# Layer 3's gated linear attention: decay product first, second values and keys turned inside the gate products, filling steps ahead of the squares' sum

## The reference

```
gate_logit = b_lr @ w_a2 + b_a2
log_a = log_sigmoid(gate_logit) / 16
b = cumsum(log_a within a chunk);  b_last, b_ref = b at the chunk's end, at its middle
qe = q * 128**-0.5 * exp(b - b_ref);  ke = k * exp(b_ref - b)
o_intra = (causal part of qe @ ke.T) @ v
chunk_kv = (k * exp(b_last - b)).T @ v
state[n+1] = exp(b_last) * state[n] + chunk_kv[n]
o = o_intra + (q * 128**-0.5 * exp(b)) @ state
b_out = rmsnorm(o) * b_norm_g * silu(b_gate)
y = concat(a_out, b_out) @ w_out
```

## Time and profile before

| | |
|---|---|
| median of 3 runs | 3675.92 us (3673.31 to 3685.54) |
| the profiled execution's own time | 3676.82 us |
| its span, first to last instruction | 3674.7 us |
| mean granted TensorE clock | 0.968 of full speed |
| TensorE busy | 3449.6 us in 16240 matmuls |
| VectorE, ScalarE, GpSimd busy | 1772.1, 1119.6, 1071.0 us |
| the four heads' part of the span | about 3067 to 3500 us |

### The profile page before, as it was taken

One profiled execution on the slowest core, in us unless ns is written; L12 is line 12 of the kernel. 1 busy time (PEld: TensorE's weight loads), 2 busy tenths in 40 slices (PEclk: granted clock), 3 DMA queues, 4 the chain that ended last, 5 costly groups with the idle time before them and its releaser, 6 DMA issues.

```text
span 3674.7 us, 39245 instructions
## 1 busy us (share of the span) xinstructions
PE 3449.6 (94%) x16240; PEld 2811.3 (77%) x16240; DVE 1772.1 (48%) x1897; ACT 1119.6 (30%) x1492; POOL 1071.0 (29%) x1144
## 2 busy tenths in 40 slices
PE   9989999999999999898898999999999999999997
PEld 7655678888887688555598989989987777777776
DVE  4567562222223688686455544545574223443522
ACT  4333352111122522444531111111243332322442
POOL 3111343323233243000023433433342222211243
PEclk9999999999999999899899999999999999999998
DMA  3000211111111211000111111111121111001232
GB/s 122 23 23 29 103 63 63 52 46 49 50 46 64 87 46 41 12 6 6 59 41 39 43 46 52 41 46 52 41 87 52 64 59 45 29 24 35 75 133 96
DMA packets 56249, 192.21 MB, mean 52 GB/s; under 512 B 6900, under 2 KB 7284, under 8 KB 55560
## 3 DMA queue, kind: packets, MB, share of 16 engines
q1 hardware_dynamic: 56072, 189.71, 15.0%
HBM read 172.83 MB, written 16.86 MB: 52 GB/s over the span
## 4 chain that ended last, share of the span: by engine, by line
PE 78%; DVE 14%; ACT 5%; issue 2%; DMA 0%; POOL 0%; DVEq 0%; ACTq 0%; SPq 0%; POOLq 0%
PE psum L270 21%; PE psum L271 21%; PE psum L272 21%; PE psum L138 11%; DVE mix L107 3%; DVE work L98 2%; PE psum L312 2%; PE psum L314 1%; PE psum L313 1%; DVE res L98 1%; DVE res L107 1%; ACT L126 1%; DVE work L116 1%; DVE u_padded L98 1%; ACT work L126 1%
## 5 line engine op out<-in xcount | busy, mean ns | idle before, releaser
L98 POOL TENSOR_TENSOR w_lo<-w_raw,w_hi 128x256 fp32r<-128x256 f32 x1140 | 1070.8, 970 | 2569.0 <-ACT w_hi L131 2569.0
L270 PE MATMUL psum<-x_hi,w_hi 128*128 128x512 f32 (+2 forms) x3264 | 1220.2, 374 | 31.0 <-issue 6.8
L271 PE MATMUL psum<-x_lo,w_hi 128*128 128x512 f32 (+2 forms) x3264 | 1179.0, 361 | 0.0
L272 PE MATMUL psum<-x_hi,w_lo 128*128 128x512 f32 (+2 forms) x3264 | 1174.9, 360 | 0.0
L131 ACT CAST w_hi<-w_raw 128x1024 fp32r<-128x1024 f32 x285 | 298.2, 1048 | 1585.0 <-PE psum L272 1521.8
L270 PEld LDWEIGHTS psum<-x_hi,w_hi 128*128 128x128 f32 x3264 | 623.0, 191 | 128.2 <-issue 34.2
L271 PEld LDWEIGHTS psum<-x_lo,w_hi 128*128 128x128 f32 x3264 | 622.3, 191 | 84.3 <-issue 19.1
L272 PEld LDWEIGHTS psum<-x_hi,w_lo 128*128 128x128 f32 x3264 | 620.9, 190 | 71.4
L270 PE MATMUL psum<-h_hi,w_hi 128*128 128x512 f32 x848 | 337.4, 398 | 15.3 <-issue 9.0
L272 PE MATMUL psum<-h_hi,w_lo 128*128 128x512 f32 x848 | 331.8, 391 | 0.0
L271 PE MATMUL psum<-h_lo,w_hi 128*128 128x512 f32 x848 | 331.8, 391 | 0.0
(11 more groups left out here) (281 smaller groups left out, 3675.6 us busy)
## 6 DMA issues: line engine op xcount, KB each, us to landing
w_raw<-w_dram SPq DMA_DIRECT2D x285, 512.0 KB, 3.2
res<-spill SPq DMA_DIRECT2D x4, 1044.0 KB, 9.5
res<-x_dram SPq DMA_DIRECT2D x8, 512.0 KB, 8.3
res<-x_dram SPq DMA_DIRECT2D x4, 1024.0 KB, 8.0
spill<-res SPq DMA_DIRECT2D x1, 4096.0 KB, 13.9
spill_a<-mix SPq DMA_DIRECT2D x8, 512.0 KB, 2.6
res<-spill_a SPq DMA_DIRECT2D x8, 512.0 KB, 4.7
x_plain<-spill SPq DMA_DIRECT2D x4, 1024.0 KB, 10.2
```

What stands on the lines that cost most here:

```text
L98: self.mark(self.e.tensor_tensor(out, a, b, op), inc)
L270: t.e.matmul(out, whi, xhi, start=k == 0, stop=False, skip_group_check=True)
L271: t.e.matmul(out, whi, xlo, start=False, stop=False, skip_group_check=True)
L272: ins = t.e.matmul(out, wlo, xhi, start=False, stop=last_k, skip_group_check=True)
```

## The change

TensorE issues a head's decay product ahead of the transposes of the first values. The second values are transposed after 32 of the 48 filling steps and the keys after 40. ScalarE has the products of a new label, ("first gate", h), ahead of its copies of the second values and keys, and the rest of the three products behind them. Of the ten steps behind the squares' sum, four stand ahead of its wait. Two functions, `uses` and `claim_banks`, are added to the core and called nowhere.

```diff
-    FILL_V, FILL_NORM, FILL_SGU, FILL_FIRST, FILL_STEP, FILL_ROOT = 4, 2, 4, 3, 2, 10
+    FILL_V, FILL_NORM, FILL_SGU, FILL_FIRST, FILL_STEP, FILL_SUM, FILL_ROOT, FILL_TURN, FILL_KEYS = 4, 2, 4, 3, 2, 4, 6, 32, 8
...
         for h in range(H3):
-            t.wait_ge(*k.products["bv", 2 * h].freed)
-            t.wait_ge(self.vt_ready, 16)
-            t.wait_ge(self.o_out, 8 * h)
-            t.wait_ge(self.state, 15 * h)
-            self.pe_turn(t, self.v_f, 3 * h)
             fill = self.pe_values_and_gates(t, h)
             t.wait_ge(self.w_a2_landed, 16)
             t.wait_ge(self.biased, 9)
             t.wait_ge(*k.products["lr",].freed)
             t.wait_ge(self.b_out, 2 * h)
             t.mm([(ps[:, 4 + i, :], self.w_a2[:, h, :], self.lr[0:16, i * 512:(i + 1) * 512], True, True) for i in range(2)], self.gate_mm)
+            t.wait_ge(*k.products["bv", 2 * h].freed)
+            t.wait_ge(self.vt_ready, 16)
+            t.wait_ge(self.o_out, 8 * h)
+            t.wait_ge(self.state, 15 * h)
+            self.pe_turn(t, self.v_f, 3 * h)
+            advance(fill, self.FILL_TURN)
+            k.label(("first gate", h))
+            t.wait_ge(*k.products["bv", 2 * h + 1].freed)
+            self.pe_turn(t, self.v_f, 3 * h + 1)
+            advance(fill, self.FILL_KEYS)
+            t.wait_ge(self.q_ready, 4 * h + 4)
+            self.pe_turn(t, self.kd, 3 * h + 2)
             drain(fill)
             k.label(("values", h))
-            t.wait_ge(*k.products["bv", 2 * h + 1].freed)
-            self.pe_turn(t, self.v_f, 3 * h + 1)
-            t.wait_ge(self.q_ready, 4 * h + 4)
-            self.pe_turn(t, self.kd, 3 * h + 2)
             self.pe_update(t, h, 0)
...
+            advance(fill, self.FILL_SUM)
             t.wait_ge(self.o_total, h + 1)
             t.wait_ge(self.masked, 16 * h + 16)
             t.mm(k.ones_of(self.ke, TWO, (4, 5)), self.o_sum)
...
-            self.act_products(a, ("values", h))
+            self.act_products(a, ("first gate", h))
             self.act_turned(a, self.v[1], 3 * h + 1)
             self.act_turned(a, self.kd_tok, 3 * h + 2)
+            self.act_products(a, ("values", h))
```

More of the change, by code:

```diff
@@ L297, in claim_at, with uses, claim_banks @@
         return p, before
+    def uses(self, *slots):
+        return [(self.slots[i], self.slot_uses[i]) for i in slots]
+    def claim_banks(self, key, first, width, cols, slot):
+        self.slot_uses[slot] += 1
+        p = Product(key, first, width, cols, self.slots[slot], self.slot_uses[slot])
+        assert key not in self.products, key
+        self.products[key] = p
+        return p
     def claim_high(self, key, at):
```

## The result

The changed kernel takes 3638.57 us as the median of 4 runs (3636.83 to 3639.46), the kernel before 3679.53 (4 runs, 3673.31 to 3685.54). The ratio is 0.9893, with a 95% interval of 0.9880 to 0.9907: 39 us, or 1.07%, faster. The forecast was 3643.5 us.

What follows compares the result with a forecast made beforehand. TensorE, busy 94% of the span, bounds the kernel. Savings 5.6 + 12.2 + 10.4 + 2.8 + 3.6 = 34.6, + 0.9 - 3.1 = 32.4 us; 3676.8 - 32.4 - 0.9 = 3643.5 us, range 3636 to 3660.

Steps and rivals of the forecast that it cites:

- Idle time (23.6 us): TensorE's waits for first values, copies of second values, copies of keys and squares' total: 5.3, 8.4, 2.9, 7.0 us.
- The clock: Slow-clock time behind waits at first filling step, first state update and squares' sum: 11.0 us, 7.9 taken as regained.
- Rival A: Only the idle time goes and the clock falls as often as now: 23.2 us gained, 3652.7 us; chance 0.22.
- Part 2: Second values' and keys' transposes inside the gate products: only 2.06 us of transposes remain there per head, 12.2 saved.
- part 1: Decay product ahead of the first values' transposes: 2.93 us for both, the wait gone, 5.6 us saved over four heads.
- Head 3: Behind its first state update: second state at 5.5 us, third update not before; 0.9 us gained through four output steps.
- (a): Second values' multiply ends before their transposes after 32 filling steps: cover 1.5 us, so no TensorE wait.
- (b): ScalarE's copies of the second values, behind the first gate's activation, end before the keys' transposes: cover 1.8 us.
- b_out: The last head's output, which the decay product waits for, is ready before the next head starts: cover 3.0 us.
- B: New waits at the transposes, two covers missed by 1 us each, and head 3's late operands: 3653.5 us; chance 0.08.
- C: Time isn't saved but moves to the next head's start, where VectorE's root chain ends late: 3674 us; chance 0.05.
- D: Slower: late ScalarE copies of second values hold the keys' transposes, each us past cover costing one per head; chance 0.03.

Runs made afterwards that it cites:

- The sevenfold transposes: The changed kernel with the keys' transposes issued seven times over in each head; 3660.58 us in one run.
- the operands first: The changed kernel with ScalarE rounding head 3's first two operands ahead of the last gate's cast and Silu; 3637.02 us, again 3638.92.
- part 2 alone: The changed kernel with first values' transposes back ahead of the decay product and all ten steps behind the squares' sum; 3664.59 us, 0.9956 of before.
- part 4 alone: The kernel before with only four of the ten steps moved ahead of the squares' sum's wait; 3666.30 us, 0.9963 of before.

## Why the prediction was right

**Idle time (23.6 us)** went as named, all four groups in full.

**The clock (11.0, of which 7.9 were taken).** Here the forecast was too careful. All of it came back in heads 0 to 2. The reason for the caution was that transposes and the decay product might bring the clock down by themselves. The sevenfold transposes answer it for the first, and 32 first filling steps without a wait and without a fall for the two together. Over the eleven profiled executions I counted the slow matmuls (0.63 us instead of 0.39) behind each place, at the squares' sum also the sum's own product (2.4 to 3.7 us instead of 1.9):

| place | falls where a wait stands ahead | falls where none does |
|---|---|---|
| first filling step (1.3 us) | 5 of 12 | 0 of 32 |
| first state update, heads 0 to 3 (2.1 and 0.7 us) | 11 of 12 | |
| first state update, heads 0 to 2 | | 0 of 24 |
| squares' sum (2.3 us) | 6 of 9 | 0 of 24 |
| head 3's third update in the changed kernels (0.6 and 1.6 us) | 5 of 6 | |
| the same with the operands first (0.6 and 0.3 us) | | 0 of 2 |

(Waits of up to 0.6 us are counted as none.) What decides whether a given wait ends in a fall, no run shows: in the kernel before it was heads 1 and 2 at the first place, in part 2 alone heads 1, 2 and 3, in part 4 alone none. So the 11.0 us are what one execution of the kernel before happened to lose, and that the forecast's size fits the medians may owe something to luck. The spread of the runs can't settle it, as the falls of unprofiled runs can't be seen: it was 12 us before, 3 in the first four runs after, and 9 when the changed kernel ran again. The extra falls of the lower bound were priced at 1.6 us by heads 0 and 1 in the earlier trace rows; these cost 1.57 and 1.99. Rival A, only idle time gone (3652.7), is out.

**The transposes.** Part 2 charged 1.03 us for eight; between steps they cost less. From the start of the filling to the update is 34.65 us where 32.82 + 2.06 = 34.88 was forecast, and part 1's decay product and transposes take 2.76, not 2.93. With the shorter chunks (34.21 for 34.36) and end (21.59 for 21.73) a head is 96.3 and not 97.1 us: 2.2 us over three heads.

**Head 3.** Forecast: second state 5.5 us behind the first update, third update not before. Measured: the state ends at 3398.11, 5.2 behind 3392.90, the update starts at 5.3. The stretch took 10.43 us, 10.27 were forecast. It is the one place where the clock still fell, behind a wait of 1.58 that the change itself made.

**The covers.** (a) The second values' multiply ends at 3185.45 in head 1 and step 32 at 3187.44: 2.0 us. In head 0 it is 3089.51 and 3091.09, so 1.6 (1.5 forecast). (b) With four steps fewer than eight the wait was 0.5, so the cover is 2.7 - 0.5 = 2.2 us (1.8). For b_out, 3256.9 against 3259.1: 2.2 us (3.0). None was missed, so rivals B, C and D fell. D's price, a us in each head for each us past the cover, was too low: 0.5 us of wait cost 0.7 a head with the keys' transposes four steps earlier, and 3.3 to 3.7 us past cover (a) cost 5.2 to 5.5 where the clock fell too.

**The sum.** 34.6 + 0.9 of the working, 0.16 less in head 3, and 2.2 of cheaper transposes and chunks make 37.5, measured 37.7; with 0.5 ahead of head 0 and 0.1 lost behind, 38.1. Against the 32.4 forecast, the mechanism was right and two sizes were off: the 3.1 us of clock kept back, of which nothing was lost in heads 0 to 2, and the 2.2 of transposes and chunks.

## What to carry to other kernels

A wait of 1.3 to 2.3 us of a TensorE that is otherwise busy may cost about twice its length (1.32 of wait and 1.57 of slow clock in head 1, 2.32 and 1.7 at its squares' sum), as the clock can fall behind it; add the slow stretches behind the waits to the waits when pricing a change. Fill a wait with steps that are due anyway until the releaser's chain has some us to spare (here 2 us), and check each queue that the moved work is put ahead of. Where the filling isn't there, as in head 3, the same reordering made new stalls of 0.6 and 1.6 us, and only a look at what stands behind what on VectorE and ScalarE showed it.

## What the runs showed of the hardware

Float32 transposes of 128x128 kept TensorE at the full clock for 6.3 us without another matmul, at 0.109 us each. Behind idle time of 3.3 to 3.7 us it was low in three cases of four, behind waits of 1.3 us in 5 of 12, of 2.3 us in 6 of 9, and of 0.5 us in none of four. After a fall the matmuls of 128x512 ran at 0.43 us start to start for 1 to 6 us and then at 0.23. Stretches that nobody edited moved by up to 5.0 us from one profiled execution to another: among the kernels with the decay product first, the first one starts at 3063.96 us in one and at 3068.93 in another, with the same work ahead of it.
